# Row dots inside three early rounds of a top-k choice, and eight of 48 scaled one-hot groups made by GpSimd

## The reference, cut to what matters

```python
s1 = jnp.einsum('nhd,hkd->nhk', q1, sub_k1)
s2 = jnp.einsum('nhd,hkd->nhk', q2, sub_k2)
v1, i1 = lax.top_k(s1, PEER_TOPK)
v2, i2 = lax.top_k(s2, PEER_TOPK)
cand = (v1[..., :, None] + v2[..., None, :]).reshape(n, PEER_HEADS, PEER_TOPK * PEER_TOPK)
top_s, top_c = lax.top_k(cand, PEER_TOPK)
e1 = jnp.take_along_axis(i1, top_c // PEER_TOPK, axis=-1)
e2 = jnp.take_along_axis(i2, top_c % PEER_TOPK, axis=-1)
idx = e1 * PEER_N_KEYS + e2
g = jax.nn.softmax(top_s, axis=-1)
act = jax.nn.gelu(jnp.einsum('nhkd,nd->nhk', e_down[idx], xb))
return jnp.einsum('nhk,nhkd->nd', g * act, e_up[idx])
```

## Time and profile before

| | |
|---|---|
| three executions | 2691.06, 2693.71, 2698.30 us |
| the profiled execution | 2692.59 us, its span 2690.8 us |
| busy over the span | PE 91%, PEld 79%, DVE 82%, POOL 50%, ACT 41% |
| the stage between the last cross attention and the expert loop | about 1188 to 1601 us |
| mean granted TensorE clock | 0.97 |

### The profile page before, as it was taken

How to read it: one execution, slowest core, us unless ns; L and a number is a source line. 1 busy time by engine, 2 the same in 40 slices (tenths; PEclk the granted TensorE clock), 3 DMA queues, 4 the chain that set the end, 5 groups by cost and what they waited for, 6 DMA issues and landing times.

```text
span 2690.8 us, 38692 instructions
## 1 busy us (share of the span) xinstructions
PE 2439.7 (91%) x13259; PEld 2116.3 (79%) x13259; DVE 2208.6 (82%) x3961; ACT 1107.1 (41%) x1938; POOL 1339.9 (50%) x1054
## 2 busy tenths in 40 slices
PE   7989999899988999999825669999999999999998
PEld 5767889788866788778614668999999999989997
DVE  6355546986688888865799979999999999999998
ACT  4453544333266223333217983333333333343333
POOL 0000000326613445634454447787777777767874
PEclk9999999999999999999867899999999999999999
DMA  6735547458954878968802359999999999999996
GB/s 240 276 119 206 182 165 289 154 195 312 365 160 149 305 285 312 349 250 339 351 0 91 161 212 416 399 414 415 415 404 400 403 398 409 404 394 386 415 413 248
DMA packets 237396, 793.77 MB, mean 295 GB/s; under 512 B 21568, under 2 KB 70768, under 8 KB 214992
## 3 DMA queue, kind: packets, MB, share of 16 engines
q0 software_dynamic: 112288, 408.77, 39.0%
q1 hardware_dynamic: 124976, 383.29, 37.9%
HBM read 731.16 MB, written 60.82 MB: 294 GB/s over the span
## 4 chain that ended last, share of the span: by engine, by line
PE 64%; DVE 19%; DMA 8%; ACT 4%; issue 3%; POOL 1%; SPq 0%; POOLq 0%; DVEq 0%; ACTq 0%
PE lin L242 14%; PE lin L243 13%; PE lin L244 13%; PE tr L242 6%; PE tr L243 6%; PE tr L244 6%; DMA row_ring<-in_down,IDX 4%; DVE w_lo L219 2%; DMA w_raw<-in_wall 2%; DVE row_ring L136 2%; DVE w_hi L1902 2%; ACT w_hi L211 1%; DVE mark L1907 1%; DVE att_nmx L1104 1%; POOL row_ring L148 1%
## 5 line engine op out<-in xcount | busy, mean ns | idle before, releaser
L148 POOL DMA_INDIRECT row_ring<-in_down,IDX x256 | 339.8, 1327 | 367.1 <-DVE dots L136 299.2
L242 PE MATMUL lin<-w_hi,T_hi 128*128 128x512 f32 x976 | 392.8, 402 | 15.0 <-DVE w_lo L219 7.0
L243 PE MATMUL lin<-w_lo,T_hi 128*128 128x512 f32 x976 | 388.8, 398 | 0.0
L219 DVE TENSOR_TENSOR w_lo<-w_raw,w_hi 128x2048 fp32r<-128x2048 f32 x94 | 216.4, 2302 | 210.0 <-ACT w_hi L211 205.9
L244 PE MATMUL lin<-w_hi,T_lo 128*128 128x512 f32 x976 | 388.5, 398 | 0.0
L136 DVE CUSTOM_DVE_ANT_0 row_ring<-row_ring,H 128x1024 f32<-128x1024 f32 x256 | 304.7, 1221 | 84.4 <-DMA row_ring<-in_down,IDX 83.0
L211 ACT ACTIVATE w_hi<-w_raw 128x2048 fp32r<-128x2048 f32 x116 | 222.0, 1914 | 368.3 <-PE lin L244 327.3
L242 PE MATMUL tr<-T_hi,w_hi 128*128 128x384 f32 x1024 | 349.3, 341 | 3.1 <-DVE w_lo L2204 3.1
L244 PE MATMUL tr<-T_hi,w_lo 128*128 128x384 f32 x1024 | 346.2, 338 | 0.0
L243 PE MATMUL tr<-T_lo,w_hi 128*128 128x384 f32 x1024 | 345.8, 338 | 0.0
L2114 POOL DMA_INDIRECT rows<-in_up,now x192 | 305.1, 1589 | 77.5 <-issue 53.0
(11 more groups left out here) (291 smaller groups left out, 5259.5 us busy)
## 6 DMA issues: line engine op xcount, KB each, us to landing
w_raw<-in_wall SPq DMA_DIRECT2D x116, 1024.0 KB
G<-in_downT SPq DMA_DIRECT2D x128, 512.0 KB
row_ring<-in_up SPq DMA_DIRECT2D x128, 512.0 KB
wd<-dense_gates SPq DMA_DIRECT2D x32, 768.0 KB
weight_rests<-w_lo SPq DMA_DIRECT2D x22, 1024.0 KB, 4.8
w_lo<-weight_rests SPq DMA_DIRECT2D x22, 1024.0 KB
dense_gates<-peer SPq DMA_DIRECT2D x6, 2048.0 KB, 6.5
dense_gates<-w_raw SPq DMA_DIRECT2D x6, 2048.0 KB, 6.9
```

Source lines behind the costliest of these rows:

```text
L148: pool.indirect_dma_start(self.ring[:, r % self.K, :], None, self.table, bass.IndirectOffsetOnAxis(ap=self.IDX[:, r:r + 1], axis=0)).then_ ...
L219: dve.tensor_tensor(self.lo[:, h % 2], self.raw[:, h % 2], self.hi[:, h % 2].bitcast(F32), ALU.subtract).then_inc(self.lo_done, 1)
L242: pe.matmul(out, lhs[0], rhs[0], start=start, stop=False, skip_group_check=True)
L243: pe.matmul(out, lhs[0], rhs[1], start=False, stop=False, skip_group_check=True)
```

## The change

Two things. First, VectorE takes 8 row dots ahead of each of the two chunks of adds in place of 5, 14 behind the norm in place of 12, then runs rounds 0, 1 and 2 with a row dot at each `aside`, and only then the rows that are left; the other rounds follow. GpSimd's issues are placed to match: it asks up to six rows ahead of those, with `more_rows` between its own steps of the first three rounds. Second, groups n = 3, 9, 15, ... 45 get no `mark1`: GpSimd makes their `hot1` by itself, 8 `tensor_scalar` (is_equal, then mult) on 128x128 from `keys` and two columns of `pairs`, behind the candidate sums and the id copy of round r for r from 9, after waits on `copied` and on `bank_ready`. ScalarE waits for that (`pool_gated`) and passes it on by raising `gated`. Further, `place_done` and `keys_done` become one semaphore, and the calls of `st.split_lo` in this part are gone.

```diff
+        begun = bg.done
...
+        BY_POOL = [n for n in range(ND * OCTS) if n % 6 in (3,)]
+        EARLY, ROWS_XO, ROWS_FIRST = 3, 8, 14
...
             def gate(i, r):
                 n = i * OCTS + r
                 act.wait_ge(stamped, n + 1)
+                if n in BY_POOL:
+                    act.wait_ge(pool_gated, BY_POOL.index(n) + 1)
+                    act.wait_ge(gated, n)
+                    act.sem_inc(gated, 1)
+                    return
...
             for c in range(2):
-                bg.dve(dve, 5)
+                bg.dve(dve, ROWS_XO)
...
+            def one_row():
+                bg.dve(dve, 1)
...
-                dve.tensor_tensor(hot2[:, r % 4], keys[:].unsqueeze(1).broadcast_to((P, OCT, NK)),
+                last = dve.tensor_tensor(hot2[:, r % 4], keys[:].unsqueeze(1).broadcast_to((P, OCT, NK)),
...
+                if n in BY_POOL:
+                    last.then_inc(stamped, 1)
+                    return
                 if n >= 2:
                     dve.wait_ge(gated, n - 1)
...
-            bg.dve(dve, 6)
-            st.split_lo(dve, H0 + 6)
-            bg.dve(dve, 6)
-            st.split_lo(dve, H0 + 7)
+            bg.dve(dve, ROWS_FIRST)
+            assert all(st.is_loaded(H0 + h) for h in range(6, 12))
+            for r in range(EARLY):
+                pick_experts(r, one_row)
             bg.finish(dve)
-            for c in range(1, NPC):
-                pick_experts(2 * c - 2)
-                if c < NPC - 1:
-                    st.split_lo(dve, H0 + 6 + 2 * c)
-                pick_experts(2 * c - 1)
-                if c < NPC - 1:
-                    st.split_lo(dve, H0 + 7 + 2 * c)
-            pick_experts(6)
-            pick_experts(7)
+            for r in range(EARLY, 8):
+                pick_experts(r)
...
-            bg.pool(pool, bg.end)
+            taken = begun + 2 * ROWS_XO + NT - 1 + ROWS_FIRST
+
+            def more_rows(n):
+                nonlocal taken
+                taken += n
+                bg.pool(pool, min(taken + bg.K, bg.end))
+
+            more_rows(0)
+
+            def gate(r):
+                for n in range(6 * (r - 9), 6 * (r - 8)):
+                    if n in BY_POOL:
+                        i, o = n // OCTS, n % OCTS
+                        pool.wait_ge(copied, i + 1)
+                        pool.wait_ge(bank_ready, 2 * n - 2)
+                        for k in range(OCT):
+                            col = OCT * o + k
+                            last = pool.tensor_scalar(hot1[:, o % 2, k, :], keys[:], pairs[:, i, 0, col:col + 1],
+                                                      pairs[:, i, 2, col:col + 1], ALU.is_equal, ALU.mult)
+                        last.then_inc(pool_gated, 1)
...
             for r in range(UNITS + 1):
                 u = r
+                if r == EARLY:
+                    bg.pool(pool, bg.end)
                 if u < UNITS:
-
+                    if r < EARLY:
+                        more_rows(4)
                     pool.wait_ge(halved, u + 1)
...
                     pool.tensor_copy(id_b[:, u % 3], ids[:, u % 2]).then_inc(ids_read, 1)
+                    if r < EARLY:
+                        more_rows(1)
+                if r >= 9:
+                    gate(r)
                 u = r - 1
...
                                        x[:, 0], x[:, 1], ALU.add).then_inc(looked_up, 1)
+                    if r < EARLY:
+                        more_rows(1)
```

More of the change, by code:

```diff
@@ L1575, in routing_and_gates @@
         gsum = m.sb("gsum", [P, NT * PH])
-        small_in, chain, place_done, keys_done = (
-            m.sem(f"rt_{x}") for x in ("small_in", "chain", "place_done", "keys_done"))
+        small_in, chain, tables_done, pool_gated = (
+            m.sem(f"rt_{x}") for x in ("small_in", "chain", "tables_done", "pool_gated"))
         halved, paired, ids_read, marked, looked_up, adding = (
@@ L1866, in pick_experts @@
                     if u == 0:
-                        dve.wait_ge(place_done, 1)
+                        dve.wait_ge(tables_done, 1)
                     if u >= 2:
@@ L1900, in stamp @@
                 if n == 0:
-                    dve.wait_ge(keys_done, 1)
-                dve.tensor_tensor(hot2[:, r % 4], keys[:].unsqueeze(1).broadcast_to((P, OCT, NK)),
+                    dve.wait_ge(tables_done, 2)
+                last = dve.tensor_tensor(hot2[:, r % 4], keys[:].unsqueeze(1).broadcast_to((P, OCT, NK)),
                                   pairs[:, i, 1, OCT * r:OCT * (r + 1)].unsqueeze(2).broadcast_to((P, OCT, NK)), ALU.is_equal)
+                if n in BY_POOL:
+                    last.then_inc(stamped, 1)
+                    return
                 if n >= 2:
@@ L1953, in _ @@
             pool.wait_ge(small_in, 64)
-            pool.tensor_copy(place[:], iota[:].unsqueeze(2).broadcast_to((P, TOPK, LOOK))).then_inc(place_done, 1)
-            pool.tensor_copy(keys_b[:], keys[:].unsqueeze(2).broadcast_to((P, NK, 2))).then_inc(keys_done, 1)
-            bg.pool(pool, bg.end)
+            pool.tensor_copy(place[:], iota[:].unsqueeze(2).broadcast_to((P, TOPK, LOOK))).then_inc(tables_done, 1)
+            pool.tensor_copy(keys_b[:], keys[:].unsqueeze(2).broadcast_to((P, NK, 2))).then_inc(tables_done, 1)
+            taken = begun + 2 * ROWS_XO + NT - 1 + ROWS_FIRST
[15 more added lines that the diff above has]
+                        last.then_inc(pool_gated, 1)
             sums = 0
```

## The result

| | median us | runs | ratio to before |
|---|---|---|---|
| before | 2693.7 | 2688.1 to 2698.3, 5 | |
| after | 2713.9 | 2712.0 to 2718.2, 5 | 1.008, 95% interval 1.0068 to 1.0093 |

Forecast were 2681 us and a range of 2663 to 2697. The kernel became 20 us slower: the forecast was wrong, in its sign too. Rival C came true in its place and its price, and with it the halved gain of part 1 that rival D had, though mostly for other causes than D's.

The account below looks back on a forecast made before the run. VectorE's idle time for row landings and the rounds' work stood one after the other; part 1 gains 24, part 2 (GpSimd's groups) loses 12, so −12 from the median 2693.7 gives 2681 us, range 2663 to 2697.

Parts of the forecast that it names:

- Rival C: Gate stage, mark of group 5 and ScalarE at group 45: slow `tensor_scalar`, 0.8 us each, loses 41 us, 2711; chance 0.12.
- part 1: Rows and early rounds ahead of round 3: VectorE's idle time filled, round 3 at 1338.6 not 1362.56, gain 24.0 us.
- rival D: Norm and rounds: late landings and look-ups starving the ring halve the early rounds' gain to 13, loss 12, 2693; chance 0.16.
- nothing behind 1601 is edited: Expert loop, from 1601 us: no edit there, so what is gained or lost before it passes to the end.
- I take c = 0.35: Gate stage: assumed price in us of one GpSimd `tensor_scalar` of 128x128, between bounds of 0.29 and 1.04.
- 8(8c − 1.3): Gate stage, seven rounds and the tail: loss from GpSimd's eight groups, c us per instruction; 12 us at 0.35.
- ScalarE, released later, has room: Gate stage: after the halt at group 3, ScalarE has 16.6 us of work in a round of 22.5 before its next wait.
- Six more early rows are not free: The two chunks of adds ahead of the norm: a TensorE stall of 2.0 us and 0.7 more, 2.7 in all.
- 14 rows, 26.0 us: Behind the norm: 14 row dots at their present pace, from 1249.3 to 1275.3.
- Rounds 0 to 2, 43.8: VectorE's first three rounds: 24.2 us of rounds plus 19.6 for 17 row dots, none waiting, to 1319.1.
- The last 13, 19.5 us: Rows left before round 3: a 4.8 us look-up partly hidden, then eight rows at 1.25 us each, to 1338.6.
- B: Gate stage: GpSimd's groups fit beside `pick` and the hot keys, saving about 4 us, 2666; chance 0.24.

Follow-up runs that it names:

- experiments 6 and 7: The changed kernel with GpSimd's `tensor_scalar` taking two constants for the two columns (2700.2 us), or leaving out the second operation, the scale (2703.2 us).
- mark_free: The changed kernel with VectorE's mark of group 5 waiting for group 1's count in place of group 3's: 2725.4 us, ratio 1.0126.
- rows_first: The changed kernel without groups by GpSimd, which issues all remaining rows in round 2 before the look-up: 2676.7 us, ratio 0.9944.
- own_buffer: The changed kernel with GpSimd's groups in their own buffer, made before the wait for the candidates, and the wait of `mark_free`: 2678.9 us, ratio 0.9954.

## Why the prediction was wrong, step by step

**What bounds the kernel, and "nothing behind 1601 is edited".** Right: the expert loop kept its length to 0.4 us, and rounds 3 to 8 to 0.1.

**"I take c = 0.35".** This step failed, and it alone turns the sign: with a right c and all of part 1 the sum is −24 + 40 = +16. Without this miss, the gain of 12.7 and the loss of 12 had come to nothing. One `tensor_scalar` takes 0.787 us undisturbed. With it, 8(8c − 1.3) gives 40.0 us, and measured are 37.7. So the mechanism is right, and the closeness is in part luck: from no instruction to eight the gates grew by 43.3 us and not by the 50.4 of the formula, and the saving at none was 5.6 and not 10.4. In the round shown, GpSimd's block and what follows it took 9.77 us (1450.49 to 1460.26), by the formula 10.6; `pick` and the hot keys held GpSimd for only 1.1 us of the 1.74 that I had added, and the last link took 2.36 in place of 2.56. With c = 0.35 it had given 12.

I had bounded c by 0.29 and 1.04 and picked the row nearest in size. Size was the wrong nearness. The copy with one input of the kernel before has 0.18 us fixed and 0.83 ns an element; experiments 6 and 7 leave about 0.52 us at 128x128 for one operation with a constant, 0.12 for the second operation and 0.08 for each column read, as worked out there. None of the three was in any row. Where a term is multiplied by 64 and its break-even, 0.54, lies inside its bounds of 0.29 to 1.04, a chance of 0.12 for the far side was too little: half of the stretch between the bounds lies above the 0.66 from which the kernel is 8 us slower. The Trainium skill's figures (GPSIMD Engine Reference, Performance versus the Vector engine), 0.29 or 0.37 as estimates, lie at less than half of the measured 0.79. The Trainium skill's advice (GPSIMD Engine Reference, Engine selection) to give elementwise work to VectorE and not to GpSimd held here. That row gives the slow two-input operations as its ground and calls those with one input roughly line-rate; this one has one input, and took 0.787 us against 0.31 on ScalarE. GpSimd's idle 72 us of the gate stage, with which I had argued against the advice, were no help: the idle time stood before the candidates (9.77 us in the round shown), and the groups stood behind them.

**"ScalarE, released later, has room".** Right at 101.8 us busy of 158.3. But `mark_free` shows that I had placed the loss too narrowly: ScalarE's order binds the round without VectorE's wait on the pass. The tail lost 5.1 us (30.3 against 25.2), about what a round did (4.7), as forecast.

**"Six more early rows are not free", 2.7 us.** Right: the norm's last product ends 58.5 us behind the tables' issue, 3.3 later than before. TensorE stalled 2.70 us at 1209.60 for an add of the first chunk, forecast 2.0, though these adds began 8.7 us late. They stood behind a wait of 11.82 us for a landing that the forecast hadn't seen: GpSimd issued that row only at 1197.20, behind its wait for the stage's tables and two conversions of them. The adds of the second chunk start at 1228.59, right behind a row dot, and the early rows gave 3.9 us net.

**"14 rows, 26.0 us".** 3.1 short: 29.1 us (1245.80 to 1274.86). The longest wait in them was 5.97 us in place of 5.19, and the fourteenth row came 2.13 us late, where before it had landed.

**"Rounds 0 to 2, 43.8".** 1.3 short: 45.1 us. "I let none of them wait" held for all rows but the first, which waited 1.74 us, and three dots lasted longer than 1.2 (1.65 us at 1298.55, 1.80 at 1304.29, 1.35 at 1307.59). That is more than the 1.3; the rest of the rounds took a little less than before.

**"The last 13, 19.5 us".** This step failed too: short by 6.4, more than half of what rival D took away. I had set a look-up of 4.8 us beside the dots as cover; it was taken from a stretch in which no dot ran beside it. In truth they hold each other: from the end of the rounds to the first row issued behind the look-up it was 13.4 us (1319.93 to 1333.34) and not 9.5, and the seven rows behind that one went at 1.6 us each and not 1.25. I had used the very same hold in part 2, for the hot keys against the candidates, and not here. `rows_first` shows what it cost to have the look-up ahead of the issues, 3.6 us. Of the 24 us then: 24.0 − 0.6 (early rows) − 3.1 (the 14 rows) − 1.3 (rounds) − 6.4 (the last 13) = 12.6, with rounding the 12.7 of the ledger.

**The rivals.** C gave 2711 for c = 0.8 with a full part 1, D gave −13 for part 1. Both numbers came: 2693.7 − 12.7 + 37.7 is 2718.7, and the profiled execution began its stage 4.2 us early. C's mechanism came with it. D's didn't, in the main: it had put the loss to the norm (up to 8 us, measured 0.6 over the forecast) and to a ring starved inside the rounds (1.3), and most of it lay in the rows behind them. That the total stands only 3 us from C's 2711 is in part luck, since C had all of part 1 in it. B fell: the groups fit only when they stand in front of the candidates in a buffer of their own, and then they gain 0.1 us, not 4.

## What to carry to other kernels

A kind of instruction that no row shows isn't priced by the row nearest in size, when it is issued 64 times and its break-even lies within the bounds: then the bounds carry the chances. An engine idle for half a stage is of use only where its idle time stands ahead of what the others wait for; look where in the round it is idle, and move the new work there, with a buffer that lets it. Here that took the loss away and brought no gain, since the work grew from 0.79 to 1.40 us apiece and the last group stood in the tail. And a cover is worked out with the duration that the covering and the covered work have beside each other, not with that of each alone.

## What the runs showed of the hardware

- GpSimd's `tensor_scalar` of 128x128 fp32 took 0.787 us with two operations and two columns as scalars, 0.637 with two constants, 0.592 with one operation and a column (the shortest of 64 each). ScalarE's scaled activation of the same size takes 0.31.
- Row dots of VectorE (128x1024 fp32, two inputs) back to back beside GpSimd's 16-bit look-up: 2.94, 2.17, 1.68 and 1.43 us in place of 1.2, and the look-up 8.4 in place of 4.8. The two lasted 8.4 us together, from 1319.74 to 1328.12; one after the other the look-up's 4.8 and the four dots' 4.6 had been 9.4, so beside each other they gained 1 us only. Neither had to wait for the whole of the other's series.
- The same `tensor_scalar` took 1.40 us in the mean when it stood beside VectorE's marks and choices (`own_buffer`), so moving 64 of them to GpSimd's idle time took 89 us of that engine for 50 of undisturbed work, and VectorE's hot keys rose from 1.205 to 1.262 us.
